# Prompt attention of three branches on pairs of heads: scores of two heads in the two row halves of TensorE, bias and masks from one table

## The reference

```
NSA_HEADS = 16; NSA_KV_GROUPS = 2; NSA_HEAD_DIM = 64; NSA_WINDOW = 512
slopes = alibi_slopes(NSA_HEADS).reshape(G, R)          # 2 ** (-8 (h + 1) / 16)

def gqa_attend(q, k, v, qpos, kpos, mask, slopes):
    s = jnp.einsum('...qgrd,...kgd->...grqk', q, k).astype(jnp.float32) * NSA_SCALE
    dist = (qpos[..., :, None] - kpos[..., None, :]).astype(jnp.float32)
    s = s - slopes[:, :, None, None] * dist[..., None, None, :, :]
    p = masked_softmax(s, mask[..., None, None, :, :])
    o = jnp.einsum('...grqk,...kgd->...qgrd', p.astype(v.dtype), v)
    return o, p

# window branch: 0 <= kpos <= qpos and qpos - kpos <= 512
```

## Time and profile before

| | us |
|---|---|
| runs | 3158.04, 3164.79, 3169.57 |
| median | 3164.79 |
| span of the profiled execution | 3163.9 |
| busy in it: TensorE, VectorE, ScalarE, GpSimd | 2792.1, 1249.9, 875.3, 124.2 |
| `nsa_prompt`, from its first load to its last VectorE instruction | 2001.1 to 2669.8 |
| its units, from the first score to the last output matmul | 2040.6 to 2669.2 |

### The profile page before, as it was taken

One profiled execution on the slowest core, in us unless ns is written; L12 is line 12 of the kernel. 1 busy time (PEld: TensorE's weight loads), 2 busy tenths in 40 slices (PEclk: granted clock), 3 DMA queues, 4 the chain that ended last, 5 costly groups with the idle time before them and its releaser, 6 DMA issues. The chain is left out here.

```text
span 3163.9 us, 69355 instructions
## 1 busy us (share of the span) xinstructions
PE 2792.1 (88%) x25382; PEld 1845.6 (58%) x25382; DVE 1249.9 (40%) x3286; ACT 875.3 (28%) x2098; POOL 124.2 (4%) x217
## 2 busy tenths in 40 slices
PE   6999888899982699799997999799999998888878
PEld 4556455666651544455466879667676765555534
DVE  3111455455546521111000000275757576666633
ACT  1111444333332010101000000164646464444400
POOL 0000000011102000000000000000000000221100
PEclk9999999999995699899987999798989898899989
DMA  4001100377753131511054766400000001777732
GB/s 174 22 12 49 29 1 1 117 222 220 227 159 48 38 133 62 211 45 41 31 157 138 231 221 190 116 2 2 2 1 2 2 2 50 224 229 219 228 123 77
DMA packets 312746, 320.72 MB, mean 101 GB/s; under 512 B 72420, under 2 KB 289940, under 8 KB 312089
## 3 DMA queue, kind: packets, MB, share of 16 engines
q1 hardware_dynamic: 226120, 233.29, 24.2%
q10 hardware_dynamic: 86290, 83.01, 8.6%
HBM read 289.15 MB, written 30.27 MB: 101 GB/s over the span
## 5 line engine op out<-in xcount | busy, mean ns | idle before, releaser
L2207 PE MATMUL bank<-cm_room 64*64 64x114 f32 (+1 forms) x4608 | 297.0, 441 | 6.6 <-DMA cm_room<-cache_nsa_kv 6.6
L2207 PEld LDWEIGHTS bank<-cm_room 64*64 64x64 f32 x4608 | 254.6, 163 | 45.9 <-DMA cm_room<-cache_nsa_kv 7.5
L2554 ACT ACTIVATE np_p<-bank,np_nmax 128x640 f32<-128x640 f32 (+7 forms) x256 | 179.3, 700 | 230.1 <-DVE np_nmax L2609 229.0
L2027 PE MATMUL bank<-cm_room 128*128 128x512 f32 (+3 forms) x576 | 224.9, 551 | 0.0
L2493 PEld LDWEIGHTS bank<-kv,np_pT 128*64 128x64 f32 x4224 | 149.3, 142 | 90.1 <-ACT np_pT L2563 42.0
L2493 PE MATMUL bank<-kv,np_pT 128*64 128x64 f32 x4224 | 185.1, 233 | 2.3 <-ACT np_pT L2563 2.2
L2609 DVE TENSOR_REDUCE np_nmax<-bank 128x1 f32<-128x640 f32 (+7 forms) x256 | 181.2, 708 | 8.8
L2479 PE MATMUL bank<-ident,np_p 128*128 128x128 f32 x1056 | 179.2, 296 | 3.7 <-ACT np_pcT L2574 3.0
L315 PE MATMUL bank<-ev_hT,ev_w 128*128 128x384 f32 (+1 forms) x576 | 173.4, 460 | 6.1 <-ACT zaT L258 6.1
L2027 PEld LDWEIGHTS bank<-cm_room 128*128 128x128 f32 (+1 forms) x576 | 103.9, 182 | 117.3 <-issue 106.4
L2563 ACT ACTIVATE np_pT<-bank 128x512 f32<-128x512 f32 (+3 forms) x384 | 160.5, 458 | 39.2 <-PE bank L2479 39.2
(11 more groups left out here) (516 smaller groups left out, 4066.2 us busy)
## 6 DMA issues: line engine op xcount, KB each, us to landing
ms_pg<-cache_mla SPq DMA_DIRECT2D x388, 144.0 KB, 2.7
ns_pg<-cache_nsa_kv SPq DMA_DIRECT2D x320, 128.0 KB, 2.8
cm_room<-cache_nsa_kv ACTq DMA_DIRECT2D x262, 128.0 KB, 4.1
cm_room<-cache_nsa_kv SPq DMA_DIRECT2D x250, 128.0 KB, 4.5
ns_pg<-cache_nsa_kv ACTq DMA_DIRECT2D x192, 128.0 KB, 3.2
ms_pg<-cache_mla ACTq DMA_DIRECT2D x124, 144.0 KB, 3.3
ev_w<-w_in_even SPq DMA_DIRECT2D x8, 768.0 KB, 10.0
cm_room<-w_in_odd SPq DMA_DIRECT2D x24, 256.0 KB, 6.9
```

The costliest lines, as they stand in the source:

```text
L2027: t = nc.tensor.matmul(bank[:n, f, 0:hi - lo], hT[:, i // 3 % 2, k, at:at + n], wt[:, k, lo:hi], start=k == 0, stop=k == KD - 1)
L2207: t = nc.tensor.matmul(out(blk)[kind * HD:(kind + 1) * HD], phi[blk * BLK:(blk + 1) * BLK, kind, x, :], rows(kind, blk, x), start=x == 0, ...
L2554: nc.scalar.activation(p[:, u % NPS, :width(u)], scores_ps(u)[:, :width(u)], ACT.Exp, bias=nmax[:, u % NST:u % NST + 1], accum_out=den[:, ...
```

## The change

`nsa_prompt` is rewritten for pairs of heads. The two heads of a pair lie in the partitions 0 to 63 and 64 to 127 of the query tile `q`, and the keys `kT2` are kept twice, once in each half. A unit is now a pair of heads (128 pair-units, index u; head-unit v = 2u or 2u + 1).

- Scores: one strip of up to four blocks at a time, a matmul of 64 rows for each of the two heads (L2481), into the two banks of one of two bank pairs. A unit of more than four blocks has two strips. There are 192 strips.
- The bias row is gone. A table `tab` holds slope times position with the masks in it, 9 blocks wide, for each head; GpSimd makes it from one constant `base` (16 instructions of 128x1152), double-buffered by pair.
- The keys are negated, so scores come out negated, and VectorE does one `tensor_tensor_reduce` per strip and head: it reads the bank and the table, adds, writes `np_p` in SBUF, and takes the minimum; it shows as an instruction and an accumulator read (L2622). The separate mask additions and the reduction are gone. ScalarE's exponent works in place in `np_p`, with scale -1.
- Finish: 1/sum and gate for both heads in one instruction of two columns each; the additions to `oall` stay one for each head.
- Compressed branch: the keys `kcp` are block-diagonal over the two heads, so that one matmul of 32 columns serves two heads (16 instead of 32 a quad); its bias and mask come from a table of 1 MB, `c_cbias`, in place of the mask of 64 KB.
- `odd_projection` transposes both groups of keys at once (2 in place of 4 transposes a tile) and writes them with 4 instructions of VectorE in place of 2; `compress` writes `kcp` with one more matmul, copy and memset. `odd_projection` no longer loads key positions.

The core of the diff (`strips`, `issued` and `begin` set the order):

```diff
@@ nsa_prompt: units and order
-    NPS, NST, NPT = 4, 8, 4
+    NPS, NST, NPT = 6, 8, 4
+        def strips(u):
+            hp, i, branch, b0, nblk = pairs[u]
+            if nblk <= 4:
+                return [(0, nblk, NBT - nblk)]
+            wide = nblk - 4
+            return [(0, wide, 4 if branch == 2 else 4 - wide), (wide, nblk, NBT - 4)]
+        def issued(v):
+            u, x = divmod(v, 2)
+            return [(u + 2, x)] if u + 2 < n and x < len(strips(u + 2)) else []
@@ nsa_prompt: SyncE, GpSimd
-                for gg in range(NG):
-                    sp.dma_start(kcp[HD:KQ, gg, :], a["c_cpos"]).then_inc(s_tab, 16)
+                sp.dma_start(base[:], a["c_base"]).then_inc(s_base, 16)
                 for quad in range(NH // QUAD):
-                    for h in range(QUAD * quad, QUAD * (quad + 1)):
-                        sp.dma_start(qT[:HD, h, :], d["qT"][h * HD:(h + 1) * HD, 0:SEQ]).then_inc(s_q[quad], 16)
+                    for hp in range(2 * quad, 2 * quad + 2):
+                        sp.dma_start(q[:, hp, :], d["qT"][hp * P:(hp + 1) * P, 0:SEQ]).then_inc(s_q[quad], 16)
                     if quad == 0:
-                        sp.dma_start(cmask[:], a["c_cmask"]).then_inc(s_tab, 16)
+                        sp.dma_start(cbias[:].rearrange("p h i n -> p (h i n)"), a["c_cbias"]).then_inc(s_tab, 16)
...
+                        nc.gpsimd.tensor_scalar(tab[:, hp % 2, x, :], base[:], -SLOPES[2 * hp + x], 1.0, ALU.mult, ALU.mult).then_inc(S["bias"], 1)
@@ nsa_prompt: TensorE
-                    for lo in range(0, w, 512):
-                        hi = min(w, lo + 512)
-                        t = nc.tensor.matmul(scores_ps(u)[:, lo:hi], qT[:KQ, h, i * P:(i + 1) * P], keys[:, lo:hi], start=True, stop=True)
+                    g = g0[u] + x
+                    if g >= 2:
+                        pe.wait_ge(S["mx"], 2 * (g - 1))
+                    lo, hi, _ = strips(u)[x]
+                    keys = kT2[:, branch - 1, 2 * hp // NR, (b0 + lo) * P:(b0 + hi) * P]
+                    for r in range(2):
+                        rows = slice(r * HD, (r + 1) * HD)
+                        t = nc.tensor.matmul(bank[:, 2 * (g % 2) + r, 0:(hi - lo) * P], q[rows, hp, i * P:(i + 1) * P], keys[rows], start=True, stop=True)
                     t.then_inc(S["sc"], 1)
...
-                        pe.wait_ge(s_tab, 64)
-                                t = nc.tensor.matmul(bank[:, f, m * NC:(m + 1) * NC], qT[:KQ, QUAD * quad + x, i * P:(i + 1) * P], kcp[:KQ, gg, :], start=True, stop=True)
+                                t = nc.tensor.matmul(out[:, :, i, :], q[:, 2 * quad + y, i * P:(i + 1) * P], kcp[:, gg, :, :], start=True, stop=True)
@@ nsa_prompt: VectorE
-                    link(V.tensor_tensor(ps[:, lo:lo + P], ps[:, lo:lo + P], c["causal"][:], ALU.add))
-                    if branch == 2 and i >= WIN // P:
-                        link(V.tensor_tensor(ps[:, 0:P], ps[:, 0:P], c["winlow"][:], ALU.add))
-                    V.tensor_reduce(nmax[:, u % NST:u % NST + 1], ps[:, :width(u)], AX, ALU.max, negate=True).then_inc(S["mx"], 1)
+                        V.tensor_tensor_reduce(out=p[:, v % NPS, lo * P:hi * P], in0=bank[:, 2 * (g % 2) + r, 0:(hi - lo) * P], in1=tab[:, hp % 2, r, t0 * P:(t0 + hi - lo) * P],
+                                               scale=1.0, scalar=-NEG if x == 0 else nmax[:, 0, v % NST:v % NST + 1], op0=ALU.add, op1=ALU.min,
+                                               accum_out=nmax[:, x, v % NST:v % NST + 1]).then_inc(S["mx"], 1)
@@ odd_projection: TensorE, VectorE
-                        for j in range(4):
-                            t = nc.tensor.transpose(bank[:HD, f, j * n:(j + 1) * n], kv[:, i, lo:lo + HD], ident[:])
+                        for j in range(2):
+                            t = nc.tensor.transpose(bank[:, f, j * n:(j + 1) * n], kv[:, i, (2 + 2 * j) * KVW:(3 + 2 * j) * KVW], ident[:])
```

More of the change, by code:

```diff
@@ L2249, in _ @@
                 pe.wait_ge(S["hidp"], 1)
-                nc.tensor.matmul(bank[:HD, 5, 0:2 * NC], phi2[:HD], hidp[:HD].rearrange("p h n -> p (h n)"), start=True, stop=True)
+                for lo in (0, HD):
+                    nc.tensor.matmul(bank[lo:lo + HD, 5, 0:2 * NC], phi2[:HD], hidp[:HD].rearrange("p h n -> p (h n)"), start=True, stop=True)
                 for gg in range(NG):
@@ L2373, in nsa_prompt @@
+        n = len(pairs)
         per = 2 * NTILE
[L2375 to L2393 removed]
@@ L2395, in chunks @@
-        def chunks(u):
-            return [(lo, min(units[u][5], lo + 4)) for lo in range(0, units[u][5], 4)]
-        def ahead(u):
-            return issued[u + 1] if u + 1 < n else []
-        first = [0]
-        for u in range(n):
-            first.append(first[-1] + len(chunks(u)))
-        def width(u):
-            return units[u][5] * P
-        def scores_ps(u):
-            lo = place[u][0]
-            size = 1 if units[u][5] <= 4 else 2
-            return bank[:, lo:lo + size, :].rearrange("p a b -> p (a b)")
@@ L2422, in nsa_prompt, with width, o_ps, task @@
+        first = [0]
+        for v in range(nv):
+            first.append(first[-1] + len(chunks(v)))
+        def width(v):
+            return pairs[v // 2][4] * P
+        def o_ps(v):
+            u, x = divmod(v, 2)
+            return bank[:, 6 + u % 2, x * HD:(x + 1) * HD]
+        def task(v):
+            u, x = divmod(v, 2)
+            hp, k = divmod(u, per)
+            return ((hp + 1) // 2 if x == 1 and hp % 2 == 1 and hp + 1 < NHP else None), k
         order = []
@@ L2433, in nsa_prompt @@
             cmp_fills(0, k)
-        for u in range(n):
-            for ci in range(len(chunks(u))):
-                order.append((("T", u, ci), "A"))
-            quad, k = task(u)
+        for v in range(nv):
+            for ci in range(len(chunks(v))):
+                order.append((("T", v, ci), "A"))
+            quad, k = task(v)
             if quad is not None:
@@ L2527, in _ @@
                     cmp(0, k)
-                for v in issued[0]:
-                    scores(v)
-                for u in range(n):
-                    for ci in range(len(chunks(u))):
-                        turn(u, ci)
-                    for v in ahead(u):
-                        scores(v)
-                    if u >= 1:
-                        for ci in range(len(chunks(u - 1))):
-                            weighted(u - 1, ci)
-                    quad, k = task(u)
+                for u, x in begin:
+                    scores(u, x)
@@ L2539, in _ @@
+                for v in range(nv):
+                    for ci in range(len(chunks(v))):
+                        turn(v, ci)
+                    for u, x in issued(v):
+                        scores(u, x)
+                    if v >= 1:
+                        for ci in range(len(chunks(v - 1))):
+                            weighted(v - 1, ci)
+                    quad, k = task(v)
                     if quad is not None:
                         cmp(quad, k)
-                for ci in range(len(chunks(n - 1))):
-                    weighted(n - 1, ci)
+                for ci in range(len(chunks(nv - 1))):
+                    weighted(nv - 1, ci)
@@ L2623, in cmp @@
+                    dve.wait_ge(S["pv"], first[2 * u + 2])
+                    ring.wait_emptied(dve, S, ("cv", hp // 2, 2 * (hp % 2) + 1))
+                    for x in range(2):
+                        h = 2 * hp + x
+                        dst = oall[:, i, h * HD:(h + 1) * HD]
+                        V.scalar_tensor_tensor(out=dst, in0=o_ps(2 * u + x), scalar=coef[:, k + x:k + x + 1], in1=dst, op0=ALU.mult, op1=ALU.add).then_inc(S["o"], 1)
                 def cmp(quad, k):
```

264 lines of the change are left out of this document (130 added, 134 removed).

## The result

The changed kernel takes **3032.7 us** (median of 4 runs, 3028.9 to 3037.8) where the kernel before took 3161.4 beside it: ratio **0.960, 95% interval 0.957 to 0.963**. The profiled run took 3033.5 us.

A forecast was written before the change was run, and what follows sets the result against it. TensorE's own instruction list, busy about 98% of the units' time, was taken to bound the stage. Terms -56 + 7 - 10.5 - 22 - 4 + 5 - 6 = -86.5 gave 3078 us, range 3040 to 3145.

The forecast's parts named there:

- scores without their gaps: TensorE's score matmuls in two row halves: three steps a strip where two heads took four, 225 to 169 us, minus 56.
- change-overs: TensorE's gaps between turn, scores and weighted: 80 us becomes 87 (77 to 95), plus 7.
- compressed scores: Compressed branch on TensorE: 32 score records in place of 64, 3.5 us in place of 7.0, three times, minus 10.5.
- clock: Work lost to the lower granted clock in the units: 20 us in place of 42, minus 22.
- waits, and VectorE at narrow units: TensorE's waits 5 us in place of 9, minus 4; VectorE at one-block pair-units and the order of queues, plus 5.
- start: Stage start: queries land about 2013, 32 records take 6.9 us, units begin near 2020 against 2026, minus 6 (minus 10 to 0).
- small edits, and all outside the stage: Edits to `odd_projection` and `compress`: zero, the former within 3 us.
- burst of four: Four output records alternating between column halves, 0.34 us, read as three steps with in-order issue and applied to a strip.
- full overlap: Rival on the scores: the halves cost two steps a strip, another 56 us off, 3022; chance 0.08.
- The wait at one-block units: Pair-units of one block: VectorE takes 1.67 us against TensorE's 1.41; 16 such units, plus 4.
- VectorE becomes the bound: Rival: VectorE's new instruction takes two cycles a column, 510 us in all, stage grows by some 35, 3113; chance 0.13.
- slower: Rival: the new instruction runs in three passes, VectorE needs 651 us and sets the stage, 3182; chance 0.06.

The follow-up runs named there:

- full-rows kernel: The changed kernel with both score matmuls of a strip on all 128 rows, so none runs beside another: 3104.1 us, ratio to before 0.981.
- head-by-head kernel: The changed kernel with compressed scores one head at a time, 32 matmuls of 16 columns a quad in place of 16 of 32: 3061.9 us, ratio 0.967.
- 64-partition kernel: The changed kernel with queries loaded head by head into 64 partitions, 16 transfers of 256 KB in place of 8 of 512 KB: 3037.0 us.

## Why the prediction was wrong, point by point

The sign was right, and so was what the edits act on. The size was not, by 45 us of span. The error is larger than that in its parts: the scores saved 56 us more than forecast, the change-overs gave 30 of it back, and that they partly cancel is luck. The measured terms are for the two profiled executions, 3163.9 and 3031.7 us; the gaps and the work are counts by the prices read above, the clock's loss is added up from the granted clock, and the waits are what is left of the units' 125.

| term, us | forecast | measured |
|---|---|---|
| scores without their gaps | -56 | -112.5 |
| change-overs | +7 | +37 |
| compressed scores | -10.5 | -10.5 |
| clock | -22 | -32.5 |
| waits, and VectorE at narrow units | -4 + 5 | -7 |
| start | -6 | -10.5 |
| small edits, and all outside the stage | 0 | +4 |
| sum | -86.5 | -132 |

- **Scores: the failed step, two row halves taken to cost three steps.** "A strip of the change is exactly such a burst of four: three steps, where two heads took four." It is two steps. 1056 blocks x 0.213 us = 225 us of work became 1056 x 0.107 = 113. The step came from rows 3: the fourth record of a burst starts 0.118 us after the first, read as two steps of 0.058. The duration of a group can't tell that from one long step, but the trace of the kernel before could, cut finer. Its timeline from 2110.0 to 2110.085, to 2110.162 and to 2110.2:

```profile
2110.06 0.28 PE L2493 MATMUL bank<-kv,np_pT 128*64 128x64 f32 x2
...
2110.06 0.28 PE L2493 MATMUL bank<-kv,np_pT 128*64 128x64 f32 x2
...
2110.06 0.34 PE L2493 MATMUL bank<-kv,np_pT 128*64 128x64 f32 x4
```

  Two records have begun within 0.025 us, and still two until 2110.162: both column halves at once, then both again, 0.11 us later. The burst of four was evidence for the full overlap, as rows 5 were. Those can be cut the same way, up to 1064.04 and up to 1064.10:

```profile
1063.83 0.38 PE L1517 MATMUL bank<-s_work,s_out 64*128 64x128 f32 x2
...
1063.83 0.49 PE L1517 MATMUL bank<-s_work,s_out 64*128 64x128 f32 x4
```

  Two float32 tiles of 64 rows begin together (7 ns apart), and the next pair 0.213 us after them, of which 0.107 is columns. So the full overlap and also the 0.106 that a burst of such tiles costs once stood in the trace of the kernel before. The rival had the right mechanism at a chance of 0.08, and its 3022 misses by 11 us since the change-overs cost more.
- **Change-overs, +7 forecast, +37 measured.** The gap between turn and scores became 0.15 as forecast. The one between scores and weighted went from 0.10 to 0.21 and was not in the forecast at all: 192 x (0.15 + 0.21 + 0.15) + 64 x 0.30 = 117 us against 80. Half of this 0.21 is the 0.106 in front of the second passes. In the full-rows kernel both gaps are back: 0.10 behind the scores, and turn's sum at 138 us.
- **Compressed branch.** Right: 21 to 11 us at full clock. **Clock**: the direction and cause were right (shorter runs of narrow matmuls, no wait behind them), the loss of 8.5 or 0 is below the 20 taken, and inside "between none and the 42 of now". The head-by-head kernel ties 10 us or more of it to the length of these runs; 17 more are the second falls of the kernel before, which are gone. That they went because the waits went is argued from rows 6 and 7 and was not tried apart.
- **VectorE.** Not the bound: busy for 301 of 504 us. The forecast's 369 is a sum of durations, and the measured durations add up to 368; the busy time is lower as successive instructions overlap. The new instruction was priced well (689 ns against 681 and 692; its 384 durations add up to 208 us against 202, with 59 ns more, which no row had told, on the 128 whose scalar is read from SBUF), its accumulator read too (32 against 38). The wait at one-block units did not show: turn waits 0.8 us in all for ScalarE's `np_p`. The rivals "VectorE becomes the bound" and "slower" fell with the row of 689 ns. The rule of the Trainium skill (Vector Engine (DVE) Microarchitecture Reference, section 7) was rightly read as not biting with one source in a bank.
- **Start.** Expected 7.9 to 12.9 us from the first issue to the first score, taken at 11.2; it was 7.1, below both ends. Both had moved the bytes at the 209 GB/s of rows 9, which is a rate of loads into 64 partitions; the queries into 128 came at 477, and the 64-partition kernel bears out that this is the cause. The other part, 32 records in place of 64, was right: 7.0 us for the 6.9 forecast. The first table cost VectorE 4.5 us of waiting for `np_tab`; it is part of the start.
- **Range.** It left full overlap outside, at 0.08, and full overlap was the true case. On the term that mattered most, rows 5 spoke for it and rows 3, as they were read, against it; with two rows at odds, both ends belonged inside. With full overlap inside, the range would have begun near 3022 and held the 3033.

## What to carry to other kernels

Score-like matmuls with a contraction of 64 belong in pairs on the two row halves: here the second cost about nothing, in float32 too, and the order of the four matmuls of a strip did not matter. Then count the changes between kinds of matmul, since each costs TensorE 0.15 to 0.21 us here; grouping the work into fewer, longer bursts, with more buffers, gave another 34 us. Where a few records decide the main term, cut the timeline until single starts show, and do not infer steps from the duration of a group.

## What the runs showed of the hardware

- Two float32 matmuls on the two 64-row halves start their passes 7 ns apart; the second passes start 0.533 us after the first with 512 columns, 0.106 more than the columns take.
- A matmul on the free half starts ahead of older ones that wait for the other half: pairs 13 ns apart with four records of one half ahead.
- Change of kind on TensorE: turn to 64-row scores 0.15 us, to 65-row or full-row scores 0.06; scores to weighted 0.21 and 0.10; weighted to turn 0.15.
- An addition of a table with a running minimum (`tensor_tensor_reduce`, float32, one source in a bank) takes as long as a plain addition: 689 ns for 512 columns against 681, and 288 for 128; with its scalar read from SBUF it took 748, and the accumulator read takes 83 ns.
- The same queries arrive 3.1 us sooner in loads of 128 partitions than in twice as many of 64: 477 GB/s against 265.
- The granted clock's falls move by run: the same units lost 8.5 us and 0 in two traces, the rest of the program 61 and 50, and 50 and 60 with the kernel before.
